# The order in which a wide matmul walks its columns, in four FFN phases

## The reference

```python
def conv_ffn(h, w_gu, conv_w, conv_b, w_down):
    gate, up = _split(h @ w_gu, [FFN_HIDDEN, FFN_HIDDEN])
    return (jax.nn.silu(causal_dwconv(gate, conv_w, conv_b)) * up) @ w_down
...
x = x + conv_ffn(rms_norm(x, ffn_norm[i]), ffn_w_gu[i], ffn_conv_w[i], ffn_conv_b[i], ffn_w_down[i])
```

## Time and profile before

| | us |
|---|---|
| median of 3 runs | 2594.73 (2594.65 to 2595.61) |
| the profiled execution, first to last instruction (span) | 2592.8 |
| TensorE busy in it | 2580.1 |
| VectorE (DVE), ScalarE (ACT), GpSimd (POOL) busy | 1793.1, 1428.5, 222.1 |
| mean granted TensorE clock, share of full speed | 0.999 |

### The profile page before, as it was taken

The page is one execution under the profiler, slowest core; times in us unless marked ns, Lnnn a source line. Parts: engine busy times, 40 slices in busy tenths (PEclk is TensorE's granted clock), DMA queues, the critical chain, the costliest instruction groups (busy, mean ns, idle before and its releaser), DMA issues.

```text
span 2592.8 us, 46151 instructions
## 1 busy us (share of the span) xinstructions
PE 2580.1 (100%) x15281; PEld 2266.8 (87%) x15281; DVE 1793.1 (69%) x2591; ACT 1428.5 (55%) x2210; POOL 222.1 (9%) x199
## 2 busy tenths in 40 slices
PE   9999999999999999999999999999999999999999
PEld 8888888888888888888888888888888888888888
DVE  8777777775677777776555686776777777775454
ACT  6677767654455555554444455675555555554443
POOL 0211111221100000000111000102200000000000
PEclk9999999999999999999999999999999999999999
DMA  6656555656556665656666676333566666656665
GB/s 210 220 195 198 196 189 195 198 173 188 191 186 188 187 193 188 189 190 185 189 189 191 191 237 198 118 98 123 180 194 187 192 190 190 187 187 188 189 190 168
DMA packets 137483, 482.05 MB, mean 186 GB/s; under 512 B 15265, under 2 KB 17313, under 8 KB 136384
## 3 DMA queue, kind: packets, MB, share of 16 engines
q1 hardware_dynamic: 134528, 467.72, 57.7%
q0 software_dynamic: 2368, 12.68, 1.4%
q10 hardware_dynamic: 512, 0.65, 0.1%
HBM read 478.80 MB, written 2.16 MB: 186 GB/s over the span
## 4 chain that ended last, share of the span: by engine, by line
PE 96%; DVE 2%; ACT 1%; issue 0%; DMA 0%; POOL 0%; ACTq 0%; DVEq 0%
PE ps L821 49%; PE ps L820 26%; PE pq L821 7%; PE po L821 4%; PE pq L820 3%; PE po L820 2%; PE po L1103 1%; DVE w_lo L1220 1%; PE pq L1089 0%; PE ps L927 0%; PE ps L881 0%; PE ps L910 0%; PE pq L838 0%; PE ps L929 0%; ACT w_hi L428 0%
## 5 line engine op out<-in xcount | busy, mean ns | idle before, releaser
L1220 DVE TENSOR_TENSOR w_lo<-raw,w_hi 128x1024 fp32r<-128x1024 f32 x900 | 1098.4, 1223 | 640.1 <-ACT w_hi L428 638.9
L428 ACT ACTIVATE w_hi<-raw 128x1024 fp32r<-128x1024 f32 x900 | 937.6, 1044 | 819.0 <-PE ps L821 709.1
L821 PE MATMUL ps<-xn,w_hi 128*128 128x512 f32 x3936 | 1370.2, 392 | 0.0
L820 PE MATMUL ps<-xn,w_lo 128*128 128x256 f32 x3936 | 1107.3, 281 | 0.3 <-DVE gpad L1229 0.2
L821 PEld LDWEIGHTS ps<-xn,w_hi 128*128 128x128 f32 x3936 | 736.5, 187 | 160.7
L820 PEld LDWEIGHTS ps<-xn,w_lo 128*128 128x128 f32 x3936 | 743.8, 189 | 4.3 <-issue 1.9
L821 PE MATMUL ps<-hid,w_hi 128*128 128x512 f32 x1408 | 488.2, 391 | 0.0
L820 PE MATMUL ps<-hid,w_lo 128*128 128x256 f32 x1408 | 394.3, 280 | 0.0
L821 PEld LDWEIGHTS ps<-hid,w_hi 128*128 128x128 f32 x1408 | 263.3, 187 | 57.7
L820 PEld LDWEIGHTS ps<-hid,w_lo 128*128 128x128 f32 x1408 | 266.1, 189 | 0.0
L821 PE MATMUL pq<-xn,w_hi 128*128 128x512 f32 x528 | 185.2, 393 | 0.0
(11 more groups left out here) (287 smaller groups left out, 2458.4 us busy)
## 6 DMA issues: line engine op xcount, KB each, us to landing
raw<-w_gu SPq DMA_DIRECT2D x352, 512.0 KB, 4.0
raw<-w_ssm_in SPq DMA_DIRECT2D x162, 512.0 KB, 3.8
raw<-w_down SPq DMA_DIRECT2D x128, 448.0 KB, 3.4
raw<-w_nsa_in SPq DMA_DIRECT2D x82, 512.0 KB, 3.9
raw<-w_ssm_out SPq DMA_DIRECT2D x64, 512.0 KB, 4.4
raw<-w_down SPq DMA_DIRECT2D x64, 512.0 KB, 3.7
raw<-w_nsa_out SPq DMA_DIRECT2D x32, 512.0 KB, 4.3
wcum<-cum_scratch POOLq DMA_DIRECT2D x8, 1024.0 KB, 7.7
```

The source lines that it names most:

```text
L428: act.activation(w_hi[:, slot, 0:n * P], raw[:, slot, 0:n * P], ACT.Copy).then_inc(unit_rounded, 1)
L820: pe.matmul(acc[:, n:2 * n], w_lo[:, slot, cols], x[:, kb, 0:n], start=(kb == 0), stop=False, skip_group_check=True)
L821: mm = pe.matmul(acc[:, 0:2 * n], w_hi[:, slot, cols], x[:, kb, 0:2 * n], start=False, stop=(kb == n_blocks - 1), skip_group_check=True)
L1220: TT(w_lo[:, slot, 0:n * P], raw[:, slot, 0:n * P], w_hi[:, slot, 0:n * P].bitcast(F32), ALU.subtract).then_inc(unit_split, 1)
```

## The change

In `blocks` the wide matmul gets a form that depends on the phase. In gu0 it is issued as two matmuls of 256 columns, left half and then right half, both with the same w_hi block. In the other three phases it stays one matmul of 512 columns, and moving operand and accumulator are walked in the same changed order: in down0 ("pairs") two columns of the left half, two of the right, and so on; in gu1 ("sixteens") sixteen of the left, sixteen of the right; in down1 ("odd pairs last") the pairs 0, 2, 4, ... of all 512 columns and then the pairs 1, 3, 5, ... All other phases are as before.

```diff
+            TAKEN = {ph["gu0"].tile0: "halves", ph["down0"].tile0: "pairs", ph["gu1"].tile0: "sixteens", ph["down1"].tile0: "odd pairs last"}
...
-                blocks(acc, x, range(k0, k0 + p.sizes[v]), slot, p.blocks, n)
+                blocks(acc, x, range(k0, k0 + p.sizes[v]), slot, p.blocks, n, taken=TAKEN.get(p.tile0))
...
+                def cut(a):
+
+                    if taken == "pairs":
+                        return a.rearrange("p (h t two) -> p t h two", h=2, two=2)
+                    if taken == "sixteens":
+                        return a.rearrange("p (h t l) -> p t h l", h=2, l=16)
+                    if taken == "odd pairs last":
+                        return a.rearrange("p (m o two) -> p o m two", o=2, two=2)
+                    return a
...
                     pe.matmul(acc[:, n:2 * n], w_lo[:, slot, cols], x[:, kb, 0:n], start=(kb == 0), stop=False, skip_group_check=True)
-                    mm = pe.matmul(acc[:, 0:2 * n], w_hi[:, slot, cols], x[:, kb, 0:2 * n], start=False, stop=(kb == n_blocks - 1),
-                                   skip_group_check=True)
+                    if taken == "halves":
+                        pe.matmul(acc[:, 0:n], w_hi[:, slot, cols], x[:, kb, 0:n], start=False, stop=(kb == n_blocks - 1),
+                                  skip_group_check=True)
+                        mm = pe.matmul(acc[:, n:2 * n], w_hi[:, slot, cols], x[:, kb, n:2 * n], start=False, stop=(kb == n_blocks - 1),
+                                       skip_group_check=True)
+                    else:
+                        mm = pe.matmul(cut(acc[:, 0:2 * n]), w_hi[:, slot, cols], cut(x[:, kb, 0:2 * n]), start=False,
+                                       stop=(kb == n_blocks - 1), skip_group_check=True)
```

More of the change, by code:

```diff
@@ L811, in gemm_unit, with blocks @@
                 pe.wait_ge(unit_split, p.unit0 + v + 1 + i * p.body)
-                blocks(acc, x, range(k0, k0 + p.sizes[v]), slot, p.blocks, n)
-            def blocks(acc, x, kbs, slot, n_blocks, n=T, quarters=False, b0=0, last=True):
+                blocks(acc, x, range(k0, k0 + p.sizes[v]), slot, p.blocks, n, taken=TAKEN.get(p.tile0))
+            def blocks(acc, x, kbs, slot, n_blocks, n=T, quarters=False, b0=0, last=True, taken=None):
+                def cut(a):
[6 more added lines that the diff above has]
+                    return a
                 for b, kb in enumerate(kbs, b0):
```

## The result

The changed kernel takes 2882.69 us (median of 4 runs, 2881.10 to 2883.55), the kernel before 2595.17 on the same chip: ratio 1.1105, 95% interval 1.1092 to 1.1118. It is slower by 287.5 us. The profiled execution has a span of 2879.4 us, 286.6 above that of before.

The account below looks back on a forecast made before the run. PE was taken to bound the kernel. On the profiled 2592.8 us, + 4.8 + 159.5 + 0 + 159.5 = + 323.8 gave 2916.6, and 1.9 us outside the span made 2918.5 (forecast 2918); range 2598 to 2950.

Parts of the forecast that it names:

- rival A: The forecast itself: in down0 and down1 each half-used 16-byte piece costs a fetch, 2918 us in all; chance 0.42.
- B: Column order is free while pairs stay whole; only gu0's halves are paid, 2599.5 us in all; chance 0.28.
- PE is the whole bound: Whole kernel: PE is 96% of the chain, so each ns on an FFN-phase wide matmul is a ns on the span.
- Odd pairs last, +159.5: down1: 256 fetches of 1.77 ns instead of 128, +226.6 ns a block, 159.5 us over 704 blocks.
- The meeting of the two rows: DVE's 1.75 ns per scattered element and PE's 1.77 ns per 16 unbroken bytes, taken as one read-port pace.
- Pairs, + 159.5: down0: 256 fetches of 1.77 ns instead of 128, +226.6 ns a block, 159.5 us over 704 blocks.
- rival D: Only one of down0 and down1 pays its 159.5 us, 2759 us in all; chance 0.08.
- Sixteens, 0: gu1: each run takes four whole pieces, so the order costs 0; upper bound 148 us.
- Rival E: gu1 pays as well, 1.77 ns on each of 31 breaks, 77 us more, 2996 us in all; chance 0.10.
- Halves, 4.8: gu0: one more matmul a block costs only its fixed 3.4 ns, 4.8 us over 1408 blocks; bounds 0 and 14.
- C: PE stalls one clock step at each new 64 bytes: 66 us in down0, 9 in down1, 2675 total; chance 0.08.
- F: Faster: alternating between the halves stops neighbouring pieces hindering each other, - 38 us, 2562 us in all; chance 0.04.

Follow-up runs that it names:

- run 1: Changed kernel with the three changed orders only on the moving operand's read, accumulator written plainly, gu0 split 384 + 128 columns: 2937.42 us.
- run 2: Changed kernel with the three changed orders only on the accumulator's write, gu0 halves with 64 of 128 weight columns: 2600.16 us.
- run 4: Changed kernel with runs of two columns at steps of 32 (gu0) and 256 bytes (down0), turns of 64 (gu1), pairs swapped within 16 bytes (down1): 3162.85 us.

## Why the prediction came out as it did

The time lies 35 us below the forecast, 2918. The mechanism of rival A, a price for each visit to a half-used piece, holds, but the sum is nearer than its terms: three were too small (halves by 14.2 us, sixteens by 18.2, odd pairs last by 4.7) and one too large (pairs, by 75.2), and that they partly cancel is luck. A's own range, 2895 to 2945, missed the 2882.7; only the wide range, which reached down to B, holds it. And gu1 did not keep its 0.347 a block, which the forecast itself had named as a sign of being wrong.

*PE is the whole bound; a ns on a wide matmul is a ns on the span.* Right: the four excesses add up to 285.7 of 286.6 us, so everything outside the four phases together moved by under 1 us.

*Odd pairs last, +159.5.* Right: 164.2. The read alone gives 579.1 of the 579.3, the write order alone gives nothing (runs 1 and 2), and a break within a piece gives nothing (run 4). Subtracting the narrow matmul and the fixed cost, (579.3 - 116.7 - 3.4) / 256 = 1.79 ns a visit, beside the 1.77 read off unbroken columns and the 1.75 of DVE's scattered read the earlier trace rows. By the timeline, where the wide matmul's own distance is 443 ns (mean of 87 blocks), it would be 1.72. That PE and DVE share one pace is not shown: DVE's elements lie 64 bytes apart, where PE pays 1.69, and PE's price runs from 1.35 to 2.21 by the order. The meeting of the two rows was partly luck; what the runs show is the price by the visit.

*Pairs, + 159.5.* The term was mis-sized: 84.3. I counted 256 fetches, as for odd pairs last. But a walk that comes back to a piece after one other visit gets part of it cheaper: (465.8 - 120.1) / 256 = 1.35 ns a visit. With four places in turn, or two places and no return, that is gone (592.9 and 606.5). I had this in rival D, all or nothing at a chance of 0.08; the truth lies halfway. 12.9 of the 119.7 ns come only when the write takes turns as well (run 1), though the write alone costs nothing; why wasn't found.

*Sixteens, 0.* A term put at nothing: 18.2 us, on the read side alone (run 1). It is no price per break: 359.8, 359.9, 359.9 and 359.7 for turns of 4, 8, 16 and 32, and 347.1 for 64. Rival E was right that sixteens pay, but its + 77 us, a fetch's time on each break, is refuted; what the 13 ns are stays open, with the surcharge of steps of 128 bytes and more.

*Halves, 4.8.* Mis-sized: 19.0, above the upper bound of 14. Two rows misled me. The narrow matmul hides a load of 128 columns within 116.7 ns, but only every other load has so short a cover; the next one has 230 ns. And the compression units' 118.8 ns, from which I took only the upper bound, were the nearer measure, and still a little low, since their loads have 120 columns. Three loads of 128 columns in a row take 120.0 ns each: the block takes 360.1 with 128 columns in the two w_hi loads, 353.6 with 120 and 350.1 with 64, and 406.7 where a matmul of 128 columns leaves its successor's load bare.

*The rivals.* B, the free order, is wrong for half-used pieces on the read side; the write order alone is free. C, a stall on each new 64 bytes, gave 66 us for pairs and 9 for odd pairs last: wrong in their order. F: no turning order was faster than the plain one (the best, turns of 128, took 346.4 and 346.8 against 346.6 and 347.0 in the same phases).

The Trainium skill ("Advanced Engine Details and Errata", section Memory Cachelines) asks for at least two hits on a 16-byte line of SBUF to absorb its latency. Read as "two are enough", it does not hold here: odd pairs last has two consecutive hits on each visit and takes 579.3 ns instead of 346.1, while four hits, or twice two without leaving the line, cost nothing. The line of 16 bytes agrees with the runs. The same section says that any non-contiguous pattern in PSUM significantly slows matmuls; with the moving operand read in plain order, three such write orders ran at 346.1 to 347.1. All of them kept two neighbouring columns together; single columns weren't tried.

## What to carry to other kernels

In this kernel's rounded float32 the moving operand of a matmul wants runs that use every 16-byte piece whole before leaving it, at steps of at most 64 bytes (32 bytes cost 3 ns a matmul, 64 nothing), or turns of 64 columns and more; turns of 4 to 32 columns between two places cost 13 ns. If a permutation is needed, try it in the accumulator, with the moving operand read in plain order: in runs of two columns and more it was free there. When the read takes turns in pairs, the same order in the write cost 12.9 ns more than a plain write. Cutting one matmul into two of 256 columns costs more than the fixed few ns, because three weight loads in a row take 120 ns each. When a term counts fetches, ask whether the access is a return: the same number of visits cost 1.35 or 1.79 ns each.

## What the runs showed of the hardware

- The distance between matmuls, read from the count in a stretch, shows what busy shares hide: PEld was 100% busy at 350.1 and at 406.7 ns a block alike.
- A visit to a 16-byte piece of the moving operand, 32-bit data, at the 2.4 GHz level, costs about the same whether 2 or 4 columns are used of it: 1.79 ns for either at a step of 32 bytes, 2.21 and 2.18 at 256. Unbroken columns take 1.77, half pieces at 64 bytes 1.69, and a piece returned to after one visit elsewhere 1.35.
- Swapping the two halves of each piece, with the walk going backwards by 8 bytes each time, is free.
- Turning between two places costs 13 ns a matmul of 512 columns for turns of 4 to 32 columns and nothing from 64 on.
